# Full-precision routing from whole transposed tokens, per-tile gather evacuation, and query/key heads with tokens on partitions, in a three-block kernel

## The chip, the cores and the metric

One core of a Trainium2 chip runs the whole kernel. The metric is the device time of one launch in microseconds, as a median of several runs.

## The reference

256 tokens of width 1024 pass through a hybrid block with experts, then two layers of feed-forward, mixer, feed-forward. What the change touches:

```python
# routing: top-1 of 4 groups, top-2 of the 4 experts in it (h = rms_norm(x), logits in float32)
grp_p = softmax(t @ wr_g + br_g);  grp_w, grp_idx = top_k(grp_p, 1)
in_grp = (t @ wr_e + br_e) picked by group;  top_l, top_e = top_k(in_grp, 2)
# rwkv mixer: within a chunk of 128 tokens a unit triangular system is solved (a matrix inverse per head)
# last mixer (16 heads of 64): q = rms_norm(q) * g_q / 8;  k = rms_norm(k) * g_k
s = q @ k.T + cum[t] - cum[s]          # cum: running sum of log_sigmoid(forget logit)
o = softmax(masked s) @ v;  o = o * sigmoid(gate);  out = o @ w_out
```

## The kernel before

Five engines run hand-written instruction lists, tied by semaphores. TensorE (PE) does the matmuls, VectorE (DVE) and ScalarE (ACT) evacuate PSUM and prepare operands, SyncE (SP) issues the weight stream, GpSimd (POOL) computes the reciprocal roots of the norms. Tokens are two tiles of 128; 1024 channels are 8 blocks of 128.

**Weights.** A unit is 128 x 2048 floats (1 MB) in a ring of five buffers. Where a product uses fp32r operands, each unit is split into a rounded high part (ACT, L759) and the rest (DVE, L1205), and each product is three matmuls: high x high, low x high, high x low. `split_channels` (L1991) gives channels on partitions, `split_tokens` (L2030) tokens on partitions; both take 48 matmuls of 256 columns per unit. Plain fp32 products are used elsewhere; in the trace each fp32 matmul is two records.

**Norms.** For each stage and token tile, DVE makes F = X times the gain (L1249, or L1247 with the root), PE transposes it (`x_turn`, L2006), ACT copies the result as `h_hi` (L814), DVE subtracts to `h_lo` (L1260). For the projections the first matmul waits for that.

**Routing** (`sparse`). PE multiplies the split router weights with `h_hi` and `h_lo`, 24 matmuls with 256 token columns, into 20 rows (L2281). ACT copies, PE transposes back (L2286), DVE adds the bias (L1559) and finds the group (to L1517). PE counts ranks (L2290 to L2294), DVE builds the slot matrix ST (L1585, L1586) and goes on to the expert choice; ACT takes two exponentials (L959, L961). Tokens are sorted into 5 tiles of 128 slots: 4 groups and one overflow tile. The gather (L2306) multiplies the halves of F (`f_hi` L954, `f_lo` L1554) by ST, 256 slots (two tiles) at a time, into banks 0 to 3; ACT and DVE evacuate both tiles of the first gather at once (L943, L1533).

**Experts.** Each tile takes 8 steps of gate and up (L2318 to L2320), Silu (ACT L970), product (DVE L1622), transpose (L2344) and down (L2333 to L2335). Per-slot weights come from PE by L2376 and are copied by DVE (L1615) after weight splits 2 and 3; the first Silu waits for them.

**The inverse.** 16 matrices of 128 x 128 in 4 groups are inverted in 6 levels, 24 jobs of 4 matrices. A job n does Q = Y M (`q_in`, L2592), masked by DVE (L1811), then M Q (`mw_in`, L2603) and, for n < 20, the transposed product for W (L2605); DVE subtracts both (L1819 for W, L1820 for M) and adds one tap of a convolution (L1780) per period. ACT is free there.

**The last mixer.** PE computes values with tokens on partitions (units c8 to c11, L2030), queries and keys with channels on partitions (c0 to c7, L1991). For each unit ACT squares (L1149) and copies (L745), PE sums the squares over heads with a matmul by a 0/1 matrix (`head_sums`, L2534), ACT takes the root (L1137), DVE the reciprocal over 128 x 512 (L1884) and the product (L1887). The forget logits (L2045 near 1705) follow the second query unit. Then 19 attention slots, one head each: scores (L2739, L2740), mask and maximum on DVE (L1938 to L1942), exponential on ACT (L1169), division on DVE (L1948 to L1952), transposes (L2748), values (L2758, L2759). A quarter of a gate unit, 12 matmuls (L2719), is put between slots. Units are guarded by `proj_free` (bank read) and `side_free` (bank 7 read).

## Time and profile before

| | us |
|---|---|
| median of 3 runs | 2071.33 (2067.37 to 2072.9) |
| the profiled execution | 2068.54 |
| its span | 2066.6 |
| PE, DVE, ACT busy | 1955.6, 1174.9, 868.8 |

Durations below are of the one profiled execution. "PEclk" is the granted clock of PE, 1.00 for 2.4 GHz and 0.50 for 1.2 GHz. A record's duration includes PE's pipeline, so the pace is read from the starts of neighbours.

### The profile page before, as it was taken

What the parts mean: (1) busy time and instruction counts of PE and PEld (TensorE: products, weight loads), DVE (VectorE), ACT (ScalarE), POOL (GpSimd) and SP (SyncE); (2) the same over time, 40 slices, a digit from 0 to 9 for tenths busy, and PEclk for the clock granted to TensorE, in tenths of its full rate; (3) what the DMA queues carried; (4) which work ended last, traced back from release to release, by engine and by line L of the source; (5) the groups of instructions that cost most, each with busy time, mean ns of one, the idle gap of its engine ahead of it and who ended that gap; (6) DMA issues with size and microseconds to landing.
All of it is one profiled execution on the core that took longest, in us unless ns stands there. A gap on an engine that the chain in (4) does not pass through costs nothing.

```text
span 2066.6 us, 23979 instructions
## 1 busy us (share of the span) xinstructions
PE 1955.6 (95%) x9978; PEld 1637.5 (79%) x9978; DVE 1174.9 (57%) x1397; ACT 868.8 (42%) x1083; POOL 42.1 (2%) x106
## 2 busy tenths in 40 slices
PE   6999999799999997999998989999999989999998
PEld 6987768678888885888888977888788878677887
DVE  4314353479888896554358834545655458645454
ACT  4313330257667674444221043444544345324443
POOL 0020000000000000000000000000000000000000
PEclk9989999899999998999999999999999989999999
DMA  8332223459899896555240004555455443107551
GB/s 342 140 123 102 86 98 143 170 222 370 327 345 344 342 350 226 186 194 187 82 143 22 1 1 182 205 186 192 179 194 186 155 151 123 61 2 274 183 183 41
DMA packets 51227, 363.76 MB, mean 176 GB/s; under 512 B 5680, under 2 KB 5808, under 8 KB 8496
## 3 DMA queue, kind: packets, MB, share of 16 engines
q1 hardware_dynamic: 50976, 360.13, 47.1%
q10 hardware_dynamic: 144, 2.10, 0.3%
q8 instruction: 80, 1.31, 0.2%
q14 instruction: 27, 0.22, 0.0%
HBM read 361.15 MB, written 1.05 MB: 175 GB/s over the span
## 4 chain that ended last, share of the span: by engine, by line
PE 86%; DVE 8%; ACT 3%; issue 1%; DMA 0%; POOL 0%; SPq 0%; POOLq 0%; DVEq 0%; ACTq 0%
PE bank L2045 8%; PE bank L2422 7%; PE bank L2424 7%; PE bank L2423 7%; PE bank L1991 5%; PE bank L2257 4%; PE bank L2447 4%; PE bank L2449 4%; PE bank L2448 4%; PE bank L2318 3%; PE bank L2320 3%; PE bank L2319 3%; PE bank L2247 3%; PE bank L2333 2%; PE bank L2335 2%; DVE w_a L1205 2%
## 5 line engine op out<-in xcount | busy, mean ns | idle before, releaser
L1205 DVE TENSOR_TENSOR w_a<-ring,w_a 128x2048 fp32r<-128x2048 f32 x221 | 504.4, 2290 | 301.6 <-ACT w_a L759 300.9
L759 ACT ACTIVATE w_a<-ring 128x2048 fp32r<-128x2048 f32 x221 | 420.6, 1912 | 162.5 <-PE bank L2449 90.7
L2422 PE MATMUL bank<-w_a,h 128*128 128x512 f32 x536 | 214.3, 400 | 11.1 <-DVE h L1260 5.6
L2424 PE MATMUL bank<-w_a,h 128*128 128x512 f32 x536 | 210.2, 392 | 0.0
L2423 PE MATMUL bank<-w_a,h 128*128 128x512 f32 x536 | 209.9, 392 | 0.0
L2045 PE MATMUL bank<-H,ring 128*128 128x256 f32 x800 | 182.6, 385 | 0.0
L1205 DVE TENSOR_TENSOR w_b<-ring,w_b 128x2048 fp32r<-128x2048 f32 x62 | 142.0, 2291 | 66.1 <-ACT w_b L759 65.5
L2045 PEld LDWEIGHTS bank<-H,ring 128*128 128x128 f32 x800 | 151.2, 192 | 26.0 <-issue 5.8
L759 ACT ACTIVATE w_b<-ring 128x2048 fp32r<-128x2048 f32 x62 | 118.6, 1913 | 45.7 <-PE bank L2449 25.8
L1991 PE MATMUL bank<-h,w_a 128*128 128x256 f32 x960 | 121.6, 289 | 7.0 <-DVE h L1260 7.0
L2422 PEld LDWEIGHTS bank<-w_a,h 128*128 128x128 f32 x536 | 101.4, 189 | 33.7 <-DVE hid L1652 6.7
L1991 PEld LDWEIGHTS bank<-h,w_a 128*128 128x128 f32 x960 | 118.3, 195 | 10.7 <-DVE h L1260 7.4
L1006 ACT ACTIVATE sil<-bank,tiny 128x256 f32<-128x256 f32 x88 | 41.8, 475 | 185.3 <-PE bank L2424 185.3
L2424 PEld LDWEIGHTS bank<-w_a,h 128*128 128x128 f32 x536 | 101.3, 189 | 21.8
L2423 PEld LDWEIGHTS bank<-w_a,h 128*128 128x128 f32 x536 | 101.7, 190 | 20.0
L745 ACT ACTIVATE arena<-bank 128x512 f32<-128x512 f32 (+2 forms) x59 | 34.0, 576 | 168.9 <-PE bank L2045 90.5
L2447 PE MATMUL bank<-w_a,hid 128*128 128x512 f32 x264 | 103.2, 391 | 0.0
L2449 PE MATMUL bank<-w_a,hid 128*128 128x512 f32 x264 | 102.8, 389 | 0.0
L2448 PE MATMUL bank<-w_a,hid 128*128 128x512 f32 x264 | 102.7, 389 | 0.0
L2318 PE MATMUL bank<-w_a,xg 128*128 128x512 f32 x244 | 98.1, 402 | 1.5 <-DVE xg L1533 1.5
L2320 PE MATMUL bank<-w_a,xg 128*128 128x512 f32 x244 | 95.8, 392 | 0.0
L2319 PE MATMUL bank<-w_a,xg 128*128 128x512 f32 x244 | 95.6, 392 | 0.0
(455 smaller groups left out, 3293.2 us busy)
## 6 DMA issues: line engine op xcount, KB each, us to landing
ring<-in_stream SPq DMA_DIRECT2D x330, 1024.0 KB, 4.9
G<-in_gains SPq DMA_DIRECT2D x15, 512.0 KB, 5.7
arena<-in_cmp_w ACTq DMA_DIRECT2D x1, 2048.0 KB, 7.9
sm<-in_small SPq DMA_DIRECT2D x1, 1582.0 KB, 13.0
con<-in_consts SPq DMA_DIRECT2D x1, 1384.0 KB, 17.7
X<-in_x SPq DMA_DIRECT2D x2, 512.0 KB, 4.0
out_x<-X SPq DMA_DIRECT2D x2, 512.0 KB, 2.6
sm<-in_small SPq DMA_DIRECT2D x1, 666.5 KB, 22.7
```

Source lines behind the costliest of these rows:

```text
L759: act.activation(w_slot(unit)[:, 0, :], ring[:, unit % RING, :], ACT.Copy).then_inc(S("w_hi"), 1)
L1205: dve.tensor_tensor(w_slot(unit)[:, 1, :], ring[:, unit % RING, :], w_slot(unit)[:, 0, :].bitcast(FP32), ALU.subtract).then_inc(S("w_lo"), 1)
L1991: ins = pe.matmul(ps, w(wp, k), xp[:, k, :], start=(a == 0 and k == 0), stop=(a == 2 and k == terms - 1))
L2045: ins = pe.matmul(ps, weights(k), src[:, k, :], start=(k == 0), stop=(k == KD - 1))
L2318: pe.matmul(bank[4][:, :], x_hi, w[0][:, k, :], start=(half == 0 and k == 0), stop=False)
L2320: ins = pe.matmul(bank[4][:, :], x_lo, w[0][:, k, :], start=False, stop=(half == 1 and k == 3))
L2422: pe.matmul(bank[4 + t][:, :], x_hi, w[0][:, k, :], start=first, stop=False)
L2423: pe.matmul(bank[4 + t][:, :], x_hi, w[1][:, k, :], start=False, stop=False)
L2424: ins = pe.matmul(bank[4 + t][:, :], x_lo, w[0][:, k, :], start=False, stop=end)
L2447: pe.matmul(ps, x_hi, w[0][:, f, d], start=(s == 0 and f == 0), stop=False)
L2448: pe.matmul(ps, x_hi, w[1][:, f, d], start=False, stop=False)
L2449: return pe.matmul(ps, x_lo, w[0][:, f, d], start=False, stop=(s == last and f == 1))
```

## The change

Names and lines are those of the kernel before.

- `keep_busy(n)` issues n fp32 matmuls of the identity into bank 1. Sixteen follow the first transposes; two stand on each side of the second tile's transposes in routing, eight ahead of the rank matmuls, six ahead of the gather; eight stand on each side of the second tile's transposes in the last mixer.
- Routing: ACT and DVE evacuate the transposed tokens in plain fp32 into `h_route`. For each token tile 8 fp32 matmuls with 20 columns give the logits with tokens on partitions; the split router weights, the copy and the transposes back are gone. `f_hi` and `f_lo` swap places in memory and are made within the norm.
- The first gather is evacuated tile by tile: tile 0 ahead of the first expert step, tile 1 after split 3 on ACT and ahead of splits 2 and 3 on DVE. DVE's copy of the slot weights also moves ahead of these splits. ACT runs a Silu on one column after the second exponential, ahead of the gather copies.
- Inverse: the product for W is replaced by four transposes of M (`w_in`), one job later, which ACT copies (`w_turned`); DVE's subtraction for W is gone.
- Last mixer: queries and keys by `split_tokens`; DVE sums squares over 64 columns into 8 values per tile row, ACT takes the root of 128 x 8, DVE the reciprocal, DVE scales out of PSUM into `q_tok`, PE turns 4 blocks (`turn_heads`), ACT copies with the gain. The forget logits move ahead of value unit c10, and their Exp and Ln into the value units. The factor 0.5 moves into the evacuation of the values, the sign into the maximum. Gate quarters 0 and 1 move behind the first scores, the last head unit is turned in slot 1, slots 1 and 2 hold two quarters, split 15 comes one slot later.

The core of the diff:

```diff
-        with nc.sbuf_tensor("f_lo", [P, TT, D], F32R) as f_lo:
+        with nc.sbuf_tensor("f_hi", [P, TT, D], F32R) as f_hi:
             pass
         H = sb("H", [P, KD, T])
-        with nc.sbuf_tensor("f_hi", [P, TT, D], F32R) as f_hi:
+        with nc.sbuf_tensor("f_lo", [P, TT, D], F32R) as f_lo:
...
+        with nc.sbuf_tensor("h_route", [P, KD, T], FP32) as h_route:
...
+                    if name == "moe":
+                        pre_sums(name, t)
+                        act.wait_ge(S("hs"), 2 * NB["moe"] + t + 1)
+                        act.activation(f_hi[:, t, :], F[:, t, :], ACT.Copy).then_inc(S("f_hi"), 1)
+                        act.wait_ge(S("x_turned"), 4 * NB["moe"] + 2 * t + 1)
+                        act.activation(h_route[:, 0:4, t * P:(t + 1) * P], tiles(bank[turn_bank("moe", t, 0)][:, :], 4), ACT.Copy)\
+                           .then_inc(S("x_route"), 1)
...
                     act.wait_ge(S("gathered"), 4 * max(i - 1, 0) + n + 1)
-                    src = bank[n][:, :].rearrange("p (k b c) -> p k b c", k=2, b=2)
-                    bufs = range(2) if i == 0 else (i % 2,)
-                    for b in bufs:
-                        half = b if i == 0 else int(i > 2)
-                        ins = act.activation(xg[:, b, 0, 2 * n:2 * n + 2, :], src[:, :, half, :], ACT.Copy)
-                    ins.then_inc(S("gat_hi"), 1)
+                    if i == 1:
+                        act.wait_ge(S("gat_lo"), n + 1)
+                    src = bank[n][:, :].rearrange("p (k b c) -> p k b c", k=2, b=2)[:, :, int(i in (1, 3, 4)), :]
+                    act.activation(xg[:, i % 2, 0, 2 * n:2 * n + 2, :], src, ACT.Copy).then_inc(S("gat_hi"), 1)
...
-                act.wait_ge(S("unit_used"), D_UNITS["w_out"] + SQUARE)
-                for t in range(TT):
-                    act.activation(f_hi[:, t, :], F[:, t, :], ACT.Copy).then_inc(S("f_hi"), 1)
-                act.wait_ge(S("route_pe"), AT["lg_full"])
-                act.activation(lg_t[0:20, :], bank[7][0:20, 0:T], ACT.Copy).then_inc(S("route_act"), 1)
                 split_at(2)
                 act.wait_ge(S("route_dve"), AT["rt_1"])
                 act.activation(g_exp, g_exp, ACT.Exp).then_inc(S("route_act"), 1)
                 act.wait_ge(S("route_dve"), AT["rt_2"])
                 act.activation(w2, w2, ACT.Exp).then_inc(S("route_act"), 1)
+                act.activation(sil_m[:, 0:1], C("ones")[:, 0:1], ACT.Silu)
                 for n in range(4):
                     gather_hi(0, n)
                 split_at(3)
+                for n in range(4):
+                    gather_hi(1, n)
...
+            for n in range(N_INV - 4):
+                act.wait_ge(S("w_full"), n + 1)
+                act.activation(mat_w[:, 4 * (n % 4):4 * (n % 4) + 4, :], tiles(bank[5 + n % 2][:, :], 4), ACT.Copy)\
+                   .then_inc(S("w_turned"), 1)
...
+            def turned_out(n):
+
+                act.wait_ge(S("side_full"), SI[f"hs{n}"] + 1)
+                act.activation(fq[:, 2 * n:2 * n + 2, :], tiles(bank[7][:, :], 2), ACT.Copy,
+                               scale=(qg8 if n < 4 else P2("kg"))[:, 0:1]).then_inc(S("side_free"), 1)
+
             for n in range(8):
                 split_ahead("c", 4 + n, C_SPLIT)
-
                 act.wait_ge(S(FULL[f"c{n}"][0]), FULL[f"c{n}"][1])
                 if n >= 2:
-                    act.wait_ge(S("side_full"), SI[f"hs{n - 2}"] + 1)
+                    act.wait_ge(S("qk_ss"), n - 1)
                 act.activation(f_sq[:, n % 2, :], bank[5 + GI[f"c{n}"] % 2][:, :], ACT.Square).then_inc(S("f_sq"), 1)
-                evac(f"c{n}", fq[:, 2 * n:2 * n + 2, :], ACT.Copy)
                 if n:
-                    head_norm(n - 1)
-                if n == 3:
-                    act.wait_ge(S("f_dve"), AT["f_abs"])
-                    act.activation(fe[0:N_FOX, :], fa[0:N_FOX, :], ACT.Exp, scale=-1.0).then_inc(S("f_act"), 1)
-                if n == 4:
-                    act.wait_ge(S("f_dve"), AT["f_one"])
-                    act.activation(fl[0:N_FOX, :], fa[0:N_FOX, :], ACT.Ln).then_inc(S("f_act"), 1)
-            head_norm(7)
+                    turned_out(n - 1)
+                act.wait_ge(S("qk_ss"), n + 1)
+                act.activation(qk_rs[:, n % 2, :], qk_ss[:, n % 2, :], ACT.Sqrt, bias=C("eps")[:, 0:1], scale=1.0 / HD)\
+                   .then_inc(S("qk_root"), 1)
...
+            def route_in(t):
+
+                if t == 1:
+                    low_tokens(0)
+                dve.wait_ge(S("x_turned"), 4 * NB["moe"] + 2 * t + 2)
+                dve.tensor_copy(h_route[:, 4:8, t * P:(t + 1) * P], tiles(bank[turn_bank("moe", t, 1)][:, :], 4))\
+                   .then_inc(S("x_route_2"), 1)
+                if t == 1:
+                    low_tokens(1)
+
+            def low_tokens(t):
+
+                if t == 0:
+                    dve.wait_ge(S("unit_used"), D_UNITS["w_out"] + SQUARE)
+                dve.wait_ge(S("f_hi"), t + 1)
+                dve.tensor_tensor(f_lo[:, t, :], F[:, t, :], f_hi[:, t, :].bitcast(FP32), ALU.subtract).then_inc(S("f_lo"), 1)
...
+                for n in range(4):
+                    gather_lo(1, n)
+                dve.wait_ge(S("route_pe"), AT["rc_full"])
+                dve.tensor_copy(rc, bank[7][:, 0:6 * N_TILES]).then_inc(S("route_dve"), 1)
                 split_at(2)
                 split_at(3)
-                dve.wait_ge(S("route_pe"), AT["rc_full"])
-                dve.tensor_copy(rc, bank[7][:, 0:6 * N_TILES]).then_inc(S("route_dve"), 1)
...
-                if n < N_INV - 4:
-                    dve.tensor_tensor(mat_w[:, four, :], mat_w[:, four, :], tiles(bank[5 + n % 2][:, :], 4), ALU.subtract)
...
+            def squares_in(n):
+
+                dve.wait_ge(S("f_sq"), n + 1)
+                dve.tensor_reduce(qk_ss[:, n % 2, :], f_sq[:, n % 2, :].rearrange("p (h d) -> p h d", d=HD), AX.X, ALU.add)\
+                   .then_inc(S("qk_ss"), 1)
+
+            def scaled_out(n):
+
+                rs = qk_rs[:, n % 2, :]
+                dve.wait_ge(S("qk_root"), n + 1)
+                link(dve.reciprocal(rs, rs))
+                if n >= 2:
+                    dve.wait_ge(S("side_full"), SI[f"hs{n - 2}"] + 1)
+                heads = lambda x: x.rearrange("p (h d) -> p h d", d=HD)
+                dve.tensor_tensor(heads(q_tok[:, n % 2, :]), heads(bank[5 + GI[f"c{n}"] % 2][:, :]),
+                                  rs.unsqueeze(2).to_broadcast([P, 8, HD]), ALU.mult).then_inc(S("proj_free"), 1)
...
-            for n in range(2, 14):
-                split("c", n)
-                if n == 7:
-                    forget_1()
-                if n >= 7:
-                    head_norm(n - 7)
-                if n == 9:
-                    forget_2()
-                if n == 11:
+            split("c", 2)
+            split("c", 3)
+            forget_1()
+            split("c", 4)
+            forget_2()
+            split("c", 5)
+            for n in range(8):
+                squares_in(n)
+                split("c", 6 + n)
+                scaled_out(n)
+                if n == 1:
                     forget_3()
...
-                    dve.tensor_reduce(neg_max[:, 2 * b:2 * b + 1], fat_s[:, b, 0:P], AX.X, ALU.max)
-                    link(dve.tensor_reduce(neg_max[:, 2 * b + 1:2 * b + 2], fat_s[:, b, P:3 * P], AX.X, ALU.max))
-                    dve.tensor_scalar(neg_max[:, 2 * b:2 * b + 2], neg_max[:, 2 * b:2 * b + 2], -1.0, None, ALU.mult)\
+                    dve.tensor_reduce(neg_max[:, 2 * b:2 * b + 1], fat_s[:, b, 0:P], AX.X, ALU.max, negate=True)
+                    dve.tensor_reduce(neg_max[:, 2 * b + 1:2 * b + 2], fat_s[:, b, P:3 * P], AX.X, ALU.max, negate=True)\
                        .then_inc(S("fmax_ok"), 1)
...
-                    link(dve.tensor_scalar(inv, inv, 0.5, None, ALU.mult))
...
+            def keep_busy(count):
+
+                for _ in range(count):
+                    pe.matmul(bank[1][:, 0:P], C("ident"), C("ident"), start=True, stop=True)
+
             pe.wait_ge(S("con_id"), 16)
             for t in range(TT):
                 x_turn("proj", t)
+            keep_busy(16)
...
+            def logits(t):
+
+                pe.wait_ge(S("x_route"), t + 1)
+                pe.wait_ge(S("x_route_2"), t + 1)
+                for k in range(KD):
+                    ins = pe.matmul(bank[2 * t][:, 0:20], h_route[:, k, t * P:(t + 1) * P], route_w[:, k, :],
+                                    start=(k == 0), stop=(k == KD - 1))
+                ins.then_inc(S("route_pe"), 1)
+
+            logits(0)
+            keep_busy(2)
             x_turn("moe", 1)
+            keep_busy(2)
+            logits(1)
 
             def sparse():
 
                 m0 = D_UNITS["moe"]
-                pe.wait_ge(S("h_lo"), HI0["moe"] + 4)
-                pe.wait_ge(S("wr_lo"), 1)
-                for a, (wp, x) in enumerate(((0, h_hi), (1, h_hi), (0, h_lo))):
-                    for k in range(KD):
-                        ins = pe.matmul(bank[7][0:20, 0:T], w_r2[:, wp, k, :], x[:, k, :], start=(a == 0 and k == 0),
-                                        stop=(a == 2 and k == KD - 1))
-                ins.then_inc(S("route_pe"), 1)
-                pe.wait_ge(S("route_act"), AT["lg_t"])
-                for t in range(TT):
-                    ins = pe.transpose(bank[6][:, 20 * t:20 * t + 20], lg_t[0:20, t * P:(t + 1) * P], C("ident")[0:20, 0:20])
-                ins.then_inc(S("route_pe"), 1)
+                keep_busy(8)
...
+                keep_busy(6)
...
+                if n >= 4:
+                    pe.wait_ge(S("w_turned"), n - 3)
                 if n >= 2:
                     pe.wait_ge(S("mw_ok"), n - 1)
                 for i in range(4):
                     q = mat_q[:, n % 2, i * P:(i + 1) * P]
                     ins = pe.matmul(bank[2 + n % 2][:, i * P:(i + 1) * P], mat_w[:, 4 * g + i, :], q, start=True, stop=True)
-                    if n < N_INV - 4:
-                        ins = pe.matmul(bank[5 + n % 2][:, i * P:(i + 1) * P], q, mat_w[:, 4 * g + i, :], start=True,
-                                        stop=True)
                 ins.then_inc(S("mw_full"), 1)
+
+            def w_in(n):
+                pe.wait_ge(S("mw_ok"), n + 1)
+                if n >= 2:
+                    pe.wait_ge(S("w_turned"), n - 1)
+                for i in range(4):
+                    ins = pe.transpose(bank[5 + n % 2][:, i * P:(i + 1) * P], mat_m[:, 4 * (n % 4) + i, :], C("ident"))
+                ins.then_inc(S("w_full"), 1)
...
+                if 2 <= n < N_INV - 2:
+                    w_in(n - 2)
...
+            keep_busy(8)
             x_turn("c", 1)
+            keep_busy(8)
             pe.wait_ge(S("h_lo"), HI0["c"] + 4)
             for n in range(2):
                 split_tokens(bank[5 + GI[f"c{8 + n}"] % 2], "c", n, range(1, 2))
+            pe.wait_ge(S("h_32"), H32["c"] + 4)
+            ps = side_begin("f")
+            w_f = P2("w_f").rearrange("p (k n) -> p k n", k=KD)
+            project(ps[0:N_FOX, 0:T], lambda k: w_f[:, k, :]).then_inc(S("side_full"), 1)
             for n in range(2, 4):
                 split_tokens(group_begin(f"c{8 + n}"), "c", n)
+
+            def turn_heads(n):
+
+                ps = side_begin(f"hs{n}")
+                pe.wait_ge(S("proj_free"), GI[f"c{n}"] + 1)
+                for c in range(2):
+                    for t in range(TT):
+                        at = t * UC + c * P
+                        ins = pe.transpose(ps[:, c * T + t * P:c * T + (t + 1) * P], q_tok[:, n % 2, at:at + P], C("ident"))
+                ins.then_inc(S("side_full"), 1)
+
             for n in range(8):
-                split_channels(group_begin(f"c{n}"), "c", 4 + n)
-                if n == 1:
-                    pe.wait_ge(S("h_32"), H32["c"] + 4)
-                    ps = side_begin("f")
-                    w_f = P2("w_f").rearrange("p (k n) -> p k n", k=KD)
-                    project(ps[0:N_FOX, 0:T], lambda k: w_f[:, k, :]).then_inc(S("side_full"), 1)
+                split_tokens(group_begin(f"c{n}"), "c", 4 + n)
                 if n:
-                    head_sums(f"hs{n - 1}", f_sq[:, (n - 1) % 2, :], "f_sq", n)
+                    turn_heads(n - 1)
...
+                if n == 1:
+                    turn_heads(7)
+                if n in (1, 2):
+                    gate_quarter(2 * n - 1)
+                    gate_quarter(2 * n)
+                elif n < 14:
+                    gate_quarter(n + 2 if n else 0)
```

## Rows read from the trace of the kernel before

**Rows 1.** The page: its head and the busy time of each engine.
```profile
span 2066.6 us, 23979 instructions
...
PE 1955.6 (95%) x9978; PEld 1637.5 (79%) x9978; DVE 1174.9 (57%) x1397; ACT 868.8 (42%) x1083; POOL 42.1 (2%) x106
```

**Rows 2.** PE's waits over the span: total us, times, longest us.
```profile
PE bank L2748 <- DVE sm L1952: 5.7, 3, 4.4
```

**Rows 3.** Timeline of PE at the start: start, us, line, tiles, count, [idle before].
```profile
19.51 13.76 PE L1991 MATMUL bank<-h,w_a 128*128 128x256 f32 x96 [7.04 <-DVE h L1260]
33.11 11.68 PE L2030 MATMUL bank<-w_a,h 128*128 128x256 f32 x96
```

**Rows 4.** Timeline of one period of the inverse, PE and DVE.
```profile
1121.39 1.06 PE L2592 MATMUL bank<-arena 128*128 128x128 f32 x8
1121.63 0.68 DVE L1819 TENSOR_TENSOR arena<-arena,bank 128x512 f32<-128x512 f32 x1
...
1124.07 1.06 PE L2592 MATMUL bank<-arena 128*128 128x128 f32 x8
```

**Rows 5.** Timeline of PE in the expert stage: ten transposes.
```profile
440.50 1.25 PE L2390 MATMUL bank<-con,ST 128*128 128x128 f32 x10
```

**Rows 6.** Timeline of PE: fp32 matmuls with 24 moving columns.
```profile
100.15 3.75 PE L2052 MATMUL bank<-sm,H 128*128 128x24 f32 x32
```

**Rows 7.** Timeline of all engines through routing.
```profile
398.69 1.22 PE L2006 MATMUL bank<-con,F 128*128 128x128 f32 x8 [2.64 <-DVE F L1249]
...
401.36 5.22 PE L2281 MATMUL bank<-h,late 128*20 128x256 f32 x24 [1.45 <-DVE h L1260]
...
407.38 0.38 DVE L1559 SCALAR_TENSOR_TENSOR sm<-bank,tiny,sm 128x20 f32<-128x20 f32 x2 [2.46 <-PE bank L2286]
...
408.59 0.17 DVE L1517 TENSOR_TENSOR sm<-sm 128x8 f32<-128x8 f32 x1
...
413.94 0.20 ACT L961 ACTIVATE sm<-sm 128x2 f32<-128x2 f32 x1 [3.62 <-DVE sm L1593]
...
419.65 0.50 PE L2318 MATMUL bank<-w_a,xg 128*128 128x512 f32 x1 [1.54 <-DVE xg L1533]
```

**Rows 8.** The chain that ended last, in order of time: the gather.
```profile
411.91 6.22 PE bank L2306 x32
```

**Rows 9.** Windows: PE, PEld, DVE, ACT, POOL busy (count), PEclk, DMA share, GB/s.
```profile
410.00:415.00 5.00, 3.36 (x15) 3.18 (x15) 3.78 (x21) 1.17 (x5) 0.00 (x0) 0.50 0.00 0
...
430.00:435.00 5.00, 4.83 (x15) 3.93 (x16) 2.46 (x3) 3.99 (x3) 0.00 (x0) 0.66 0.17 70
```

**Rows 10.** Timeline of the first expert step, ACT and PE.
```profile
427.76 1.28 ACT L970 ACT_TABLE_LOAD   x1 [7.15 <-PE bank L2320]
...
430.17 0.66 PE L2344 MATMUL bank<-con,mid_m 128*128 128x128 f32 x2 [2.49 <-DVE mid_m L1622]
```

**Rows 11.** Timeline of PE in the last mixer.
```profile
1674.43 19.76 PE L2030 MATMUL bank<-w_a,h 128*128 128x256 f32 x144 [2.17 <-DVE h L1260]
...
1716.99 6.31 PE L1991 MATMUL bank<-h,w_a 128*128 128x256 f32 x48
...
1723.60 6.31 PE L1991 MATMUL bank<-h,w_a 128*128 128x256 f32 x48
...
1749.57 1.02 PE L2534 MATMUL bank<-arena,con 128*128 128x512 f32 x2
...
1821.92 1.69 PE L2719 MATMUL bank<-h,w_a 128*128 128x256 f32 x12
...
1826.89 1.69 PE L2719 MATMUL bank<-h,w_a 128*128 128x256 f32 x12
```

**Rows 12.** Groups by form, DVE in the last mixer: busy us, mean ns | idle.
```profile
L1884 DVE RECIPROCAL arena<-arena 128x512 f32<-128x512 f32 x8 | 26.8, 3348 | 3.4 <-ACT arena L1137 3.4
```

**Rows 13.** Windows of the end of the inverse, columns as in rows 9.
```profile
1172.00:1176.00 4.00, 2.89 (x22) 2.32 (x20) 3.96 (x8) 0.00 (x0) 0.00 (x0) 1.00 0.00 0
1176.00:1180.00 4.00, 3.15 (x17) 3.11 (x18) 3.86 (x10) 0.24 (x1) 0.00 (x0) 0.72 0.01 4
```

86 lines of the change are left out of this document (35 added, 51 removed).

## The prediction

> **What bounds the kernel now.** I read the page first, then who TensorE (PE) waited for, then the stretches that the diff touches, instruction by instruction. PE is busy 1955.6 of 2066.6 us [rows 1], 95%, so two things can shorten the kernel: fewer PE instructions where PE never pauses, and fewer or warmer pauses where it does. Weight splitting on ScalarE (ACT) and VectorE (DVE) fills the feed-forward and expert stages, but PE hardly waits there, and the diff leaves their steady state alone. The edits lie in five places: the first projection, routing, the first expert tile, the triangular inverse in the second mixer, and queries and keys plus the attention start in the last mixer. In the last one DVE is late: PE waits 5.7 us for one DVE line [rows 2].
>
> **Prices used everywhere.** At the full clock a 128x256 fp32r matmul is issued every 0.12 us (96 in 11.68) [rows 3]. An fp32 matmul of 128 columns appears as two records of 0.112 us: in the inverse 24 records take 2.68 us [rows 4]. A transpose of 128 columns is one record, 10 in 1.25 us with the drain, 0.11 each [rows 5]. A 24-column fp32 matmul is also two records, 32 in 3.75 us with the drain, 0.11 each [rows 6]. At the half clock a 256-column matmul takes 0.22 us (24 in 5.22) [rows 7], and so does a 128-column fp32 record (estimate, twice 0.112).
>
> **The first projection.** 16 filler matmuls are put between the transposes and the wait for the split input. PE sat idle 7.04 us there and then ran 96 matmuls in 13.76 us where the next 96 took 11.68 [rows 3]: 2.1 us went to a half-speed start. The fillers take 16 x 0.22 = 3.6 us at full clock and 16 x 0.43 = 6.9 us at half clock, both inside the 7.04, so they delay nothing. Whether the clock stays up across the rest of the wait (up to 3.4 us) is open; the bounds are 0 and -2.1. I take **-1.5**.
>
> **Routing.** Before, after the second token tile's transposes at 398.69, PE waits for the split, issues 24 matmuls at half clock (401.36, 5.22 us), a copy and a transpose follow, and DVE has logits at 407.38 [rows 7]. After, tile 0's logits come in the shadow before 398.69: 16 records x 0.11 = 1.8 us from the end of the projection, and two fillers. For tile 1 ACT squares X (1.05 us) and copies F (1.0) while PE transposes, then evacuates a half (0.6); DVE subtracts one tile of F (1.2), evacuates the other half (0.6) and is done at 400.6. Eight matmuls take 1.8 us, so logits are there at 402.7 instead of 407.38: -4.6. The copies of F, once 2 us behind the transposes on ACT, are thereby moved ahead of ACT's evacuation; DVE's second subtraction sits behind its own evacuation and ends before the logits. The eight fillers before the rank matmuls end at 404.5; the group choice, 1.4 us after the first logits op in both kernels, is ready at about 404.1, so they cost 0.4. The rank matmuls and the slot comparison, 3.3 us from 408.59 [rows 7] to 411.91 [rows 8], give 407.3 for the start of the gather (-4.6). Six more fillers (1.3 us) lie in the slot comparison's 1.6 us.
>
> **Gather and first step.** The gather is 32 matmuls in 6.22 us from 411.91 [rows 8], mostly at half clock (0.50 over 410 to 415 [rows 9]); at full clock it is 32 x 0.12 = 3.7 us and ends at 411.0. Evacuation of one tile, not two, halves each copy. But a load of the Silu table (1.28 us, as at 427.76 [rows 10]) now stands on ACT between the weight exponential and the gather copies. The exponential ran at 413.94, 2.0 us after the gather's start [rows 7]; so 409.3, table to 410.9, four copies of 0.33 to 412.3, DVE's last subtraction 412.7. The first expert matmul, at 419.65 before [rows 7], comes at 412.8: **-6.9**. Then the second tile's four evacuations, and the weights' copy, stand ahead of two weight splits on DVE (2.2 us each). These splits end at 422.5, and the product DVE owes PE is behind them at 423.0; PE's transposes come 10.2 us after the first expert matmul, where they came 10.5 after it (430.17 against 419.65 [rows 7, 10]). So the moved table load buys only another 0.3 there: DVE is late next in ACT's place. DMA issue resumes some 3 us later relative to PE; its cover is the full ring, by which the DMA engines were busy for only 0.17 of 430 to 435 [rows 9]; without that cover up to 3 us come back. Sum for routing and the first step: **-7.1**, bounds -4 (fillers and gather at half clock) and -9.5 (the half-clock phase after 430 also goes).
>
> **The inverse.** A period is 24 records, 2.68 us (1121.39 to 1124.07), and DVE is full as well, with 0.60 for the W subtraction in it (1121.63) [rows 4]. After: 8 + 8 records and 4 transposes, 20 x 0.112 = 2.23; DVE 2.71 - 0.60 = 2.11; ACT one 0.6 us copy, for which it has no other work. PE becomes the bound by 0.12. That is 0.45 x 19 periods = 8.5, plus 8 records at half clock in the first (1.7), less 4 records added in one late period (0.45), plus 0.6 because DVE no longer trails PE at the end: **-10.4**. The new wait (W of job n-4 turned and copied) has two periods of room for 0.6 + 0.2 us. Bounds: -7.5 (half the DVE saving lost to hand-overs) and -11.5.
>
> **Last mixer.** (a) Eight fillers on either side of the second tile's transposes. 144 matmuls took 19.76 us [rows 11], 17.3 at 0.12: -2.4. The fillers take 1.8 us and the wait ended by the split lasts 2.17 us [rows 11] and the one ahead of the transposes about as long, so no delay. (b) A unit of queries or keys costs 48 x 0.12 in either form; the fp32 sum over 512 columns (2 records of 0.42) becomes four transposes (0.45). Units start every 6.60 us before [rows 11] and every 6.2 after; with the forget-gate stall of 0.5 gone that is -3.0. Hidden: DVE's reduce 0.7 + split 2.2 + reciprocal 0.2 + product 0.7 + waits, 4.8 us, inside PE's next unit of 5.76; it was 3.35 for a wide reciprocal, 0.75 and 2.2 [rows 12]. (c) From the end of the eighth unit (1749.57) to that of the last gate quarter (1826.89 + 1.6) PE took 79.0 us [rows 11], with one wait of 4.4 for DVE in it [rows 2], a shorter one for a split before, and some 5 us at half clock behind them. After: slot 0 costs 0.45 + 3.6, slots 1 and 2 5.5 each (two quarters, the last head turn), then 11 slots of 4.97 [rows 11]: 69.7, so -9.3. What was late there was DVE: two reciprocals of 3.35 us and two splits before the third slot. Now DVE takes up slot 0 at +4.9 us, while PE has 9.6 us of work before its next demand on it. Dropping two 0.17 us operations per slot counts only at the end, 0.3. Sum: **-15.1**, bounds -10 ((c) only half) and -17.
>
> **Sum.** -1.5 - 7.1 - 10.4 - 15.1 = -34.1. The profiled execution took 2068.5 (span 2066.6 and 1.9 around it), giving 2034.4; the median of the shown runs is 2.8 above that execution, giving 2037.2. I forecast **2036**.
>
> **A rule against it.** The granted clock fell after 1176 (0.72 over 1176 to 1180), behind gaps of PE, while 1172 to 1176, with PE at 2.89 of 4 us, ran at 1.00 [rows 13]. The Trainium skill, TensorE: Matmul & The Clock Gate, part 4 (PE-mode transpose), says that transposes don't count as TensorE activity in the same way as matmuls; by it the inverse would show less activity than its busy share. No row here has a long mix of transposes and matmuls, so the trace neither confirms nor refutes it.
>
> **Rivals.**
> 1. Fillers don't hold the clock (0.25 with the attention start good). Then the first projection gives 0, routing -4, (a) nothing: 1.5 + 3.1 + 2.4 = 7 us less gain, **2043**. For it: fillers and 20-column matmuls load PE lightly, and no row shows a clock held by such. Against: pauses shrink to under 1 us.
> 2. The attention start stays late (0.15): the new chain Square, reduce, root, reciprocal, product, turn spans three engines and one split, and if one link exceeds 5.8 us each unit stalls, and DVE reaches slot 0 late. (c) is lost: **2045**; with rival 1, 2052 (0.05).
> 3. Slower (0.03): the inverse falls to half clock and stays there. Matmuls are then 16 of its 20 records, 1.79 of 2.23 us, 80% against the 72% of 1172 to 1176 that kept 1.00 [rows 13]; it decides if transposes count for nothing and 80% is too little. Twenty periods of 20 x 0.22 instead of 2.23 us cost 43, so **2079**.
> 4. Clock luck all the way, the phase after 430 included (0.07): **2029**.
> The change could also fail to do what it says (PE bound by DVE in the inverse, so no gain from fewer records), but DVE loses 0.60 there too; it is in the bound of -7.5.
>
> **Chances.** Forecast 0.45 (2031 to 2041), rivals 0.25, 0.15, 0.05, 0.03, 0.07. The range 2028 to 2049 leaves out rivals 3 and the double case and a little of each end. Against 2071.3, faster by over 0.3% (about what a measurement can tell from no change) means under 2065: 0.94; same 0.03; slower 0.03.
>
> **What would show it.** Logits ready 4 us or so after F; 32 gather matmuls in under 4 us at clock 1.0; expert stage starting 6.9 us earlier relative to F; inverse period 2.23 on PE; unit period 6.2; no wait of PE for DVE in the first four attention slots. Wrong if fillers end after what they wait beside, if the inverse shows 0.5, or if new waits for ACT's copies appear.

## The result and the profile after

The changed kernel takes 2040.84 us (median; single executions 2036.78 to 2044.43) against 2072.11 us for the kernel before beside it (2067.37 to 2077.0): a ratio of 0.9847, 95% interval 0.9821 to 0.9873, so 1.3 to 1.8% or 26 to 37 us faster. The forecast was 2036, with 2028 to 2049. The profiled execution has a span of 2042.6 us and stands near the upper end of its kernel, as the profiled one of before stood near the lower end of its own.

The page of the changed kernel: head and busy time, as [rows 1].

```profile
span 2042.6 us, 24047 instructions
...
PE 1953.9 (96%) x10020; PEld 1641.3 (80%) x10020; DVE 1136.5 (56%) x1350; ACT 874.3 (43%) x1098; POOL 43.0 (2%) x106
```

PE's busy time has hardly changed: it includes the fillers. DVE has lost 38 us. The rows below are timelines of the changed kernel (start, duration, engine, line, operation, tiles, count and, in brackets, the idle time before and who ended it). First projection, against [rows 3]:

```profile
12.43 4.55 PE L2099 MATMUL bank<-con 128*128 128x128 f32 x32
19.57 13.25 PE L2016 MATMUL bank<-h,w_a 128*128 128x256 f32 x96 [2.58 <-DVE h L1269]
32.65 11.68 PE L2055 MATMUL bank<-w_a,h 128*128 128x256 f32 x96
```

Routing, gather and first expert step, against [rows 7, 8, 10]:

```profile
404.49 1.09 PE L2031 MATMUL bank<-con,F 128*128 128x128 f32 x8 [0.41 <-DVE F L1258]
...
408.42 0.24 DVE L1577 SCALAR_TENSOR_TENSOR sm<-bank,tiny,sm 128x20 f32<-128x20 f32 x1 [0.84 <-PE bank L2310]
...
412.92 0.38 PE L2342 MATMUL bank<-ST,f_hi 128*128 128x256 f32 x1 [0.20 <-DVE ST L1604]
...
415.17 1.28 ACT L962 ACT_TABLE_LOAD   x1
...
418.51 0.50 PE L2354 MATMUL bank<-w_a,xg 128*128 128x512 f32 x1 [1.24 <-DVE xg L1556]
```

A period of the inverse, against [rows 4]; L2651 is the four transposes, L1101 ACT's copy:

```profile
1122.54 1.06 PE L2630 MATMUL bank<-arena 128*128 128x128 f32 x8
1123.44 1.06 PE L2643 MATMUL bank<-arena 128*128 128x128 f32 x8
1124.33 0.60 PE L2651 MATMUL bank<-con,arena 128*128 128x128 f32 x4
...
1124.97 0.60 ACT L1101 ACTIVATE arena<-bank 128x512 f32<-128x512 f32 x1 [1.63 <-PE bank L2651]
```

The last mixer, against [rows 11]: L2763 turns a finished query or key unit.

```profile
1697.79 6.00 PE L2055 MATMUL bank<-w_a,h 128*128 128x256 f32 x48
1703.62 0.60 PE L2763 MATMUL bank<-con,arena 128*128 128x128 f32 x4
1703.98 6.00 PE L2055 MATMUL bank<-w_a,h 128*128 128x256 f32 x48
1711.35 0.63 PE L2763 MATMUL bank<-con,arena 128*128 128x128 f32 x4 [1.38 <-DVE arena L1913]
...
1736.15 0.60 PE L2763 MATMUL bank<-con,arena 128*128 128x128 f32 x4
...
1804.34 1.69 PE L2778 MATMUL bank<-h,w_a 128*128 128x256 f32 x12
```

The 4.4 us wait for DVE's division [rows 2] is gone; the one wait that is new is the 1.38 us before the transposes at 1711.35.

**Stages.** The program is the same in all but the edited places, so one can read each stage as the distance between two PE instructions that every kernel has. All distances are in us, from the starts in the PE timeline of each kernel's one trace. The medians and ratios come from all its executions. From the third row on the kernels are those of the experiments below. P: first matmul of the projection to the next group. R: second tile's transposes in routing to the gather. G: gather to the first expert matmul. A: first to second transposes of the second mixer. I: first job of the inverse to the first product behind it. M: second transposes of the last mixer to the first of the next stage.

| kernel | median | ratio (95%) | P | R | G | A | I | M |
|---|---|---|---|---|---|---|---|---|
| before | 2072.11 | | 13.6 | 13.2 | 7.7 | 9.1 | 73.8 | 191.1 |
| changed | 2040.84 | 0.9847 (0.9821 to 0.9873) | 13.1 | 8.4 | 5.6 | 11.9 | 63.1 | 176.7 |
| whole_again | 2043.91 | 0.9865 (0.9846 to 0.9885) | 13.1 | 10.1 | 5.6 | 12.0 | 63.3 | 177.9 |
| routing_alone | 2065.70 | 0.9962 (0.9949 to 0.9976) | 13.4 | 8.4 | 5.6 | 11.9 | 74.1 | 190.9 |
| inverse_alone | 2061.24 | 0.9943 (0.9926 to 0.9959) | 13.5 | 13.2 | 8.5 | 11.9 | 63.0 | 190.9 |
| mixer_alone | 2053.94 | 0.9920 (0.9903 to 0.9937) | 13.0 | 13.1 | 8.2 | 11.9 | 73.7 | 176.7 |
| quarters_only | 2068.61 | 0.9993 (0.9978 to 1.0009) | 13.4 | 13.1 | 8.4 | 11.9 | 73.9 | 190.8 |
| turn_by_matmul | 2048.85 | 0.9891 (0.9865 to 0.9918) | 13.1 | 11.0 | 5.2 | 11.9 | 72.4 | 176.7 |
| splits_first | 2042.63 | 0.9864 (0.9844 to 0.9883) | 13.1 | 8.4 | 5.6 | 11.9 | 63.0 | 176.7 |
| no_preload | 2037.29 | 0.9852 (0.9833 to 0.9870) | 13.1 | 8.4 | 5.3 | 9.1 | 62.1 | 176.8 |
| no_fillers | 2048.23 | 0.9889 (0.9872 to 0.9906) | 14.0 | 10.8 | 7.1 | 11.9 | 63.0 | 178.8 |
| no_fillers_again | 2051.23 (one) | | 14.1 | 10.7 | 7.3 | 11.9 | 63.0 | 178.8 |
| filled_gaps | 2036.24 | 0.9836 (0.9818 to 0.9853) | 11.6 | 10.9 | 5.3 | 9.1 | 61.6 | 176.7 |
| mended | 2030.15 | 0.9802 (0.9781 to 0.9822) | 11.6 | 11.0 | 5.2 | 9.1 | 61.8 | 175.2 |

The kernel before had a median of 2072.45 beside whole_again and the three `_alone` kernels, of 2068.53 beside no_fillers, filled_gaps, no_preload and splits_first, and of 2071.97 beside mended, turn_by_matmul, quarters_only and no_fillers_again. Medians should be compared within such a set.

### The profile page after: what moved, and what is told of

Same layout as the page of the kernel before. It is cut to its first block, busy times and chain, and to the rows that moved or that the text cites. A ratio compares the mean times of both kernels' runs of the same rounds, so it can differ in the third digit from the quotient of the medians.

```text
span 2042.6 us, 24047 instructions
## 1 busy us (share of the span) xinstructions
PE 1953.9 (96%) x10020; PEld 1641.3 (80%) x10020; DVE 1136.5 (56%) x1350; ACT 874.3 (43%) x1098; POOL 43.0 (2%) x106
## 4 chain that ended last, share of the span: by engine, by line
PE 75%; DVE 6%; ACT 3%; issue 1%; POOL 0%; POOLq 0%; DVEq 0%; ACTq 0%
PE bank L2460 8%; PE bank L2462 8%; PE bank L2461 8%; PE bank L2288 4%; PE bank L2487 4%; PE bank L2485 4%; PE bank L2486 4%; PE bank L2070 3%; PE bank L2354 3%; PE bank L2356 3%; PE bank L2355 3%; PE bank L2278 3%; PE bank L2055 3%; PE bank L2369 2%; PE bank L2371 2%; PE bank L2370 2%
## 5 line engine op out<-in xcount | busy, mean ns | idle before, releaser
L746 ACT ACTIVATE arena<-bank 128x512 f32<-128x512 f32 (+2 forms) x51 | 29.2, 573 | 172.5 <-PE bank L2070 91.8
L2055 PE MATMUL bank<-w_a,h 128*128 128x256 f32 x672 | 85.0, 288 | 2.6 <-DVE h L1269 2.6
L1672 DVE SCALAR_TENSOR_TENSOR hid<-bank,tiny,sil 128x256 f32<-128x256 f32 x88 | 42.3, 480 | 80.6 <-ACT sil L1009 80.6
```

## Experiments

**1. Each part by itself, and the whole once more.** The three parts of the diff are separate edits: inverse_alone has those of the inverse, mixer_alone those of the last mixer with its fillers, routing_alone those of routing, gather and first expert step with theirs.

```diff
 # inverse_alone, on the kernel before
-                    if n < N_INV - 4:
-                        ins = pe.matmul(bank[5 + n % 2][:, i * P:(i + 1) * P], q, mat_w[:, 4 * g + i, :], start=True,
-                                        stop=True)
...
+                if 2 <= n < N_INV - 2:
+                    w_in(n - 2)
```

> The kernel before with the new inverse alone (transposes and ScalarE's copies in place of the second product). Theory A (TensorE is bound by its records there): the period falls from 2.68 to 2.23 us, 19 times, and the kernel gains 8 to 11.5 us. Rival (transposes count less, the clock falls to the half): the granted clock shows 0.5 in the middle of the inverse, and the kernel loses some 30 us or more. Rival (the new wait for ScalarE's copy binds): period of 2.4 us or more with idle time of TensorE ahead of the products, gain below 5 us.

> The kernel before with the new last mixer alone, its sixteen filler matmuls included. Theory A: unit period 6.2 instead of 6.60 us, no wait of TensorE for VectorE in the first attention slots, the stretch from the end of the eighth unit to the last gate quarter 9 us shorter, first 144 matmuls in 17.3 us: gain 13 to 17 us. Rival (attention start stays late): units start every 6.2 us but TensorE still waits 4 us or more before the third slot: gain 6 to 9 us.

> The kernel before with routing, gather and first expert step changed alone, fillers there included, none elsewhere. Theory A: from the second token tile's transposes to the first expert matmul 14.0 us instead of 20.96, the gather in 3.7 to 4.1 us: gain 5 to 9 us. Rival (fillers do not hold the clock): the gather at clock 0.5 takes over 5.5 us, gain 3 to 4 us.

Measured: 11.2 (inverse_alone), 18.5 (mixer_alone) and 6.8 us (routing_alone) less than the kernel before beside them. The stages touched show 10.8 (I), 14.3 (M) and 6.9 (R and G, 14.0 instead of 21.0). Theory A holds for inverse_alone and routing_alone. For mixer_alone it holds in the trace, but the gain of the medians lies 1.5 us above its range, and no trace shows where the 4 us beyond M are: of the 15.2 us between the two profiled executions M accounts for 14.3. The three gains add up to 36.5 us, while whole_again, measured beside them, gained 28.5. So a median of some executions is no better than a few us as the price of one part, and the stages are the better measure. The 40 us in the middle of the new inverse in inverse_alone, as windows (busy time of PE, PEld, DVE, ACT, POOL with counts, granted clock, DMA share, GB/s):

```profile
1125.00:1165.00 40.00, 40.00 (x362) 40.00 (x361) 38.81 (x73) 10.75 (x18) 0.00 (x0) 1.00 0.01 1
```

The granted clock is 1.00, that is 2.4 GHz, all through, and so it is in the changed kernel over the same window; rival 3 is out.

> The changed kernel once more, unaltered. The profiled execution of it took 10 us more than my sum gives for it, and nearly all of that lies in stretches whose code the change does not touch (100 to 118, 300 to 310, 372 to 376, 790 to 806 and 997 to 1004 us), where TensorE ran at the half clock and did not in the profile of before. Theory A (chance: which of these stretches are slow differs from execution to execution of one kernel): in the new profile at least two of the five are at the full clock, the times of single executions spread over 7 us or so (2036 to 2044), and the gain over before is 28 to 36 us. Theory B (the change shifts the work and thereby slows these places each time): the same five stretches are slow again, within a microsecond, and the gain is 24 to 28 us.

The changed kernel again took 2037.66 to 2045.44 us. These are windows over some stretches whose code is the same in every kernel (columns as above); first the changed kernel's first trace, then its second. By 1000 us the second trace is 8 us ahead, so that its stretch for 997 to 1004 is 989 to 997 (also at half clock, not shown).

```profile
102.00:110.00 8.00, 8.00 (x43) 8.00 (x44) 0.00 (x0) 0.21 (x1) 0.00 (x0) 0.57 0.75 314
372.00:376.00 4.00, 4.00 (x13) 3.17 (x12) 0.47 (x1) 1.91 (x1) 0.00 (x0) 0.57 0.40 160
792.00:806.00 14.00, 8.53 (x25) 6.27 (x24) 7.32 (x9) 4.53 (x8) 2.34 (x6) 0.51 0.00 1
997.00:1004.00 7.00, 6.31 (x31) 5.91 (x30) 2.11 (x3) 3.50 (x8) 1.19 (x4) 0.51 0.00 0
1106.00:1120.00 14.00, 9.60 (x42) 9.13 (x43) 11.50 (x21) 0.00 (x0) 0.00 (x0) 0.51 0.00 1
```

```profile
102.00:110.00 8.00, 8.00 (x69) 8.00 (x69) 0.00 (x0) 0.81 (x2) 0.00 (x0) 1.00 0.70 291
372.00:376.00 4.00, 4.00 (x20) 3.54 (x19) 1.09 (x1) 0.00 (x0) 0.00 (x0) 1.00 0.00 0
792.00:806.00 14.00, 11.64 (x47) 9.38 (x48) 7.06 (x9) 6.43 (x11) 2.32 (x6) 0.77 0.18 66
```

The places of 102, 300 (not shown) and 372 are at full clock this time and that of 792 in part: theory A for those. The same program is at half clock in one execution and at full clock in the next. Over the first of these places that makes 3.0 us (from the 24-column matmuls to the next transposes 25.1 us, then 22.1), and the time from the first projection to routing comes out at 366.4 to 375.3 us over the fourteen traces. That of 997 is slow again, as theory B said, but not because the change shifts the work: the stage A is 11.9 or 12.0 in every trace of a kernel without fillers ahead of it but two, before's and no_preload's, with 9.1, and 11.9 in quarters_only, whose code is the old one up to the last mixer. So the trace of before, on which the forecast rests, was lucky there by 2.8 us.

**2. Who sets the period of the inverse.**

```diff
-                    ins = pe.transpose(bank[5 + n % 2][:, i * P:(i + 1) * P], mat_m[:, 4 * (n % 4) + i, :], C("ident"))
+                    ins = pe.matmul(bank[5 + n % 2][:, i * P:(i + 1) * P], mat_m[:, 4 * (n % 4) + i, :], C("ident"), start=True,
+                                    stop=True)
```

> The changed kernel with the four transposes per job of the inverse issued as fp32 matmuls by the identity: the same data, 8 records instead of 4, VectorE's and ScalarE's part unchanged. Theory A (TensorE's records set the period): the period is 24 records, 2.68 us, and the whole gain of the inverse but what VectorE's end gives is lost, 8 us slower than the changed kernel. Rival (taking the subtraction off VectorE is what shortened the period): 2.3 us or so, within 2 us of the changed kernel.

The timeline of PE, and of DVE as far as it waits:

```profile
1130.79 1.06 PE L2630 MATMUL bank<-arena 128*128 128x128 f32 x8
1131.68 1.06 PE L2643 MATMUL bank<-arena 128*128 128x128 f32 x8
1131.94 0.69 DVE L1831 TENSOR_TENSOR arena<-bank,con 128x512 f32<-128x512 f32 x1 [0.36 <-DVE arena L1800]
1132.58 1.06 PE L2651 MATMUL bank<-con,arena 128*128 128x128 f32 x8
...
1133.47 1.06 PE L2630 MATMUL bank<-arena 128*128 128x128 f32 x8
```

The period is 2.68 us again (1130.79 to 1133.47), and DVE now has an idle 0.36. The stage is 72.4 us, 9.3 more than with transposes and 1.4 less than before. PE's records set the period. The 1.4 lie behind the last period, and not all of them are DVE's: 0.55 are a shorter wait for DVE (the last two of the products M Q start 1.57 us apart, in the kernel before 2.12), and 0.8 come from the stage's last 16 small matmuls, which take 2.00 us at full clock and took 2.87 in the kernel before, where the clock fell during them [rows 13]. What else the freed DVE time is worth is room: DVE has 2.71 us of work in a period before, and with that much it could not follow a period of 2.23.

**3. The start of the attention.** The new order of the gate's quarters on the kernel before (split 15, one slot later, is not shown):

```diff
-            gate_quarter(0)
-            gate_quarter(1)
...
-                if n < 14:
-                    gate_quarter(n + 2)
+                if n in (1, 2):
+                    gate_quarter(2 * n - 1)
+                    gate_quarter(2 * n)
+                elif n < 14:
+                    gate_quarter(n + 2 if n else 0)
```

> The kernel before with the changed order of the gate's quarters and of the last weight split alone (two quarters behind the first scores, two each in slots 1 and 2); queries, keys and their roots as before. Theory A (the wide reciprocals and splits make VectorE late, not the order): TensorE still waits 3 us or more for VectorE in the first four slots and the stretch from the last unit to the next stage's transposes shortens by less than 3 of 10.5 us. Rival (the order does it): no wait above 1 us, and 6 us or more of the 10.5.

```profile
1765.21 0.55 PE L2746 MATMUL bank<-con,sm 128*128 128x128 f32 x3 [0.44 <-DVE sm L1952]
1765.52 3.12 PE L2719 MATMUL bank<-h,w_a 128*128 128x256 f32 x24
1773.63 0.90 PE L2746 MATMUL bank<-con,sm 128*128 128x128 f32 x3 [2.92 <-DVE sm L1952]
```

PE still waits 0.44 and 2.92 us for the division in the second and third slots, and M is 190.8: the order alone is worth 0.3 of 14.4 us. The 3 us that the expectation asked for a single wait was just missed, but the gain is nowhere near the rival's 6 us: DVE was late. (No run has the new queries and keys with the old order, so whether they need the new one is open.) DVE's groups in the changed last mixer (busy, mean ns) show what went, against 3348 ns each in [rows 12]:

```profile
L1902 DVE TENSOR_REDUCE tiny<-arena 128x8 f32<-128x512 f32 x8 | 5.4, 680 | 18.7 <-ACT arena L1161 18.7
L1909 DVE RECIPROCAL tiny<-tiny 128x8 f32<-128x8 f32 x8 | 1.6, 194 | 0.0
```

**4. First expert step.** Once the early Silu is left out, once DVE's order is put back:

```diff
 # no_preload
-                act.activation(sil_m[:, 0:1], C("ones")[:, 0:1], ACT.Silu)
 # splits_first
+                split_at(2)
+                split_at(3)
                 for n in range(4):
                     gather_lo(1, n)
                 dve.wait_ge(S("route_pe"), AT["rc_full"])
                 dve.tensor_copy(rc, bank[7][:, 0:6 * N_TILES]).then_inc(S("route_dve"), 1)
-                split_at(2)
-                split_at(3)
```

> The changed kernel without the one-column Silu ahead of the gather's evacuation. Theory A (the load of the table, 1.28 us, only changes places, and VectorE is late next anyway): the first expert matmul comes 0.6 to 1.0 us earlier, the first transposes of the experts stay within 0.5 us of where they were relative to the gather, total within 1.5 us of the changed kernel. Rival (the load on ScalarE is on the path of the first product): the first transposes come 1.3 us later relative to the gather.

> The changed kernel with VectorE's two weight splits again ahead of the second tile's subtractions and of the copy of the per-slot weights. Theory A (the first Silu waits for that copy, so the order decides): the first transposes of the experts come 1 to 2.5 us later relative to the gather, and so does all behind them. Rival (VectorE's sum of work ahead of the product is the same in either order): the first transposes stay within 0.5 us.

The first Silu of the experts (in no_preload the table load ahead of it), what ACT waited for there, and the first transposes, in the changed kernel, in splits_first and in no_preload:

```profile
428.20 0.47 ACT L973 ACTIVATE sil_m<-bank,tiny 128x256 f32<-128x256 f32 x1 [7.55 <-PE bank L2356]
...
429.31 0.44 PE L2380 MATMUL bank<-con,mid_m 128*128 128x128 f32 x2 [1.21 <-DVE mid_m L1642]
```

```profile
428.36 0.47 ACT L973 ACTIVATE sil_m<-bank,tiny 128x256 f32<-128x256 f32 x1 [7.57 <-PE bank L2356]
...
429.48 0.44 PE L2380 MATMUL bank<-con,mid_m 128*128 128x128 f32 x2 [1.21 <-DVE mid_m L1642]
```

```profile
420.00 1.28 ACT L972 ACT_TABLE_LOAD   x1 [7.30 <-PE bank L2355]
...
422.41 0.58 PE L2379 MATMUL bank<-con,mid_m 128*128 128x128 f32 x2 [2.49 <-DVE mid_m L1641]
```

From the gather's start to these transposes: 16.39 us, 16.42 with the splits first, 17.40 without the early load. So the order on DVE is worth nothing here (theory A of that run fell, its rival holds): in the changed kernel the Silu waits for PE's own gate and up matmuls, not for the weights' copy. The early load is worth 1.0 us net, 1.3 at the first Silu less 0.3 at the first expert matmul; there the rival was nearer than theory A. That no_preload is yet the quicker of the two by its median (2037.29 against 2042.63 for splits_first beside it) is not explained by its edit: in its one trace the stages A (9.1) and I (62.1), which it doesn't touch, are shorter.

All three have PE at the half clock during the gate and up matmuls (the changed kernel from 424 to 427 us, granted clock 0.50). In the two traces without fillers of experiment 5 these matmuls run at full clock, and there the order of arrival turns round. The same place in no_fillers:

```profile
428.23 0.47 ACT L973 ACTIVATE sil_m<-bank,tiny 128x256 f32<-128x256 f32 x1 [5.75 <-PE bank L2356]
429.79 0.48 DVE L1642 SCALAR_TENSOR_TENSOR mid_m<-bank,tiny,sil_m 128x256 f32<-128x256 f32 x1
430.32 0.44 PE L2380 MATMUL bank<-con,mid_m 128*128 128x128 f32 x2 [2.19 <-DVE mid_m L1642]
```

The Silu is done at 428.7, but DVE comes out of its second split only at 429.8, without a pause, and the transposes come 10.2 us after the first expert matmul. In the changed kernel DVE waits 0.49 us for the Silu. So DVE is late at full clock, and what no_preload and splits_first show holds for the half clock only; neither was tried at full clock.

**5. The fillers.**

```diff
-                for _ in range(count):
+                for _ in range(0):
```

> The changed kernel with all its filler matmuls left out, all else equal. Theory A (the fillers hold the clock where they stand, and lie in waits): the gather and the last mixer's first 144 matmuls come back to the half clock in most executions (1.2 to 3.4 us each), the first projection loses 0.5 us: 3 to 6 us slower than the changed kernel, at 2044 to 2050. Rival (the clock falls or holds there by chance, whether or not fillers stand in the gaps): within 1.5 us of the changed kernel, 2040 to 2044, and a similar number of half-clock stretches in routing and in the last mixer.

> The changed kernel without fillers once more, for a second trace. Theory A (they hold the clock where they stand): the gather again takes 6 us or more from its start's own wait to the first expert matmul (7.1 us instead of 5.6), and a half-clock stretch follows the transposes of the last mixer. Rival (chance): at least one of the two places is at the full clock this time.

Without fillers G is 7.1 and 7.3, M 178.8 both times; with them G is 5.2 to 5.6 in eight traces of eight, M 176.7 or 176.8 in six of the seven with the changed kernel's mixer. P is 13.0 to 14.1 in the seven traces without the sixteen at the start and 13.1 in the five with them. That is theory A, at two executions without. Of the 1.5 us that the fillers win in G, 0.6 are lost right behind it: the half-clock stretch that stands 10 us later without them now meets the gate and up matmuls, and the first transposes come 10.8 instead of 10.2 us after the first expert matmul. R is mixed: 8.4 in four traces with fillers, 10.1 to 11.0 in four, 10.7 and 10.8 without. Against splits_first beside it, whose stages match the changed kernel's, no_fillers is 5.6 us slower by the medians (the intervals of their ratios, from 0.9872 and up to 0.9883, overlap a little).

Where R is 10.9 or 11.0, the clock fell during the fillers, and the fillers themselves came too late. In turn_by_matmul:

```profile
405.16 2.88 PE L2099 MATMUL bank<-con 128*128 128x128 f32 x16
...
409.83 2.91 PE L2099 MATMUL bank<-con 128*128 128x128 f32 x12
...
411.28 0.28 DVE L1604 TENSOR_SCALAR ST<-sm 128x128 fp32r<-128x128 f32 x1
...
412.39 0.56 PE L2342 MATMUL bank<-ST,f_hi 128*128 128x256 f32 x1
```

The slot matrix was ready at 411.56, the gather started 0.8 us later, behind twelve records that take 1.58 us at full clock (411.13 in the changed kernel). filled_gaps and mended show the same.

**6. More of them.** filled_gaps puts fillers where PE waits longest (the second argument is the bank that they write):

```diff
-            keep_busy(16)
+            keep_busy(26)
...
                 scatter(N_TILES - 1)
+                keep_busy(18, 4)
                 x_turn("ffn0", 0)
...
+                    keep_busy({"ab": 8, "c": 15}.get(then, 0), 4)
                     x_turn(then, 0)
...
+            keep_busy(14, 4)
             pe.wait_ge(S("gram_free"), N_MAT)
...
+                if n == 1:
+                    keep_busy(11, 4)
...
+            keep_busy(19, 4)
             pe.wait_ge(S("gn_y"), 1)
...
+            keep_busy(22, 4)
             pe.wait_ge(S("y_rw"), 1)
```

> The changed kernel with further fillers in the longest waits of TensorE that have none: 10 more ahead of the first projection, 18 after the experts, 8 and 15 ahead of the first transposes of the second and last mixer, 14 and 11 around the first job of the inverse, 19 and 22 ahead of the mixer's output. In every trace so far a half-clock stretch follows these waits (792 to 806, 997 to 1004, 1106 to 1120, 1222 to 1236, 1649 to 1656 us in the changed kernel: 3.4 to 8.5 us each at the half clock or twice that long). Theory A (a wait makes the clock fall, a filled wait doesn't): most of them go, 10 to 20 us faster than the changed kernel, 2022 to 2032. Rival (fillers of 128 columns are too light, or the clock falls anyway): no change of the stretches and 0 to 3 us slower through fillers that end late.

mended moves the 19 behind the transposes that follow and cuts the forget gate's DVE work in two:

```diff
+                if n == 1:
+                    forget_3a()
+                if n == 2:
+                    forget_3b()
```

> The changed kernel with the further fillers of the run before, the 19 that stood too early (they ran for 4.4 us while the wait they were for, 5.1 us, lay behind the next transposes) moved behind those transposes, and with VectorE's forget-gate arithmetic cut in two, one half after the second and one after the third query unit. Theory A: the mixer from the inverse's end to the next transposes comes back to 83 to 84 us, the wait of 1.38 us for VectorE before the third unit's transposes goes, no half-clock stretch at 792 to 806, 997 to 1004, 1106 to 1120 and 1649 to 1656: 2029 to 2034. Rival (what the fillers gain in one place is lost in another, since the clock falls somewhere anyway): 2035 to 2040.

Windows of mended over the places after the filled waits, and its start (timeline):

```profile
790.00:806.00 16.00, 12.58 (x75) 10.39 (x74) 8.79 (x10) 6.31 (x11) 3.08 (x8) 1.00 0.17 51
988.00:1006.00 18.00, 16.09 (x139) 15.36 (x138) 5.80 (x8) 5.08 (x11) 2.63 (x8) 1.00 0.02 4
1098.00:1113.00 15.00, 12.74 (x110) 12.19 (x110) 14.62 (x27) 1.20 (x2) 0.00 (x0) 1.00 0.00 1
```

```profile
12.44 6.70 PE L2104 MATMUL bank<-con 128*128 128x128 f32 x52
19.65 11.78 PE L2021 MATMUL bank<-h,w_a 128*128 128x256 f32 x96 [0.51 <-DVE h L1269]
```

The clock is 1.00 where the changed kernel's two traces have the half clock for much of the time. filled_gaps gains 32.3 us over the kernel before beside it. That is 6.4 more than splits_first, but only 1.0 more than no_preload in the same set, and its median of 2036.24 lies outside theory A's range; the interval of its ratio overlaps the changed kernel's, so that its gain over the changed kernel is not clear of noise. It is less than theory A's 10 to 20: with the 19 misplaced fillers the way from the inverse's end to the next stage's transposes takes 87.5 us for 84.4, and half-clock stretches at 1157 to 1164 and 1854 to 1857 (granted clock in its trace) take some back. mended, at 0.9802, beats both kernels: the one before by 42 us beside it, the changed one by 10.7 us on medians of different sets of runs (the intervals of the ratios, up to 0.9822 and from 0.9821, just meet). It has both the moved fillers and the cut DVE work, and only the latter has a price of its own, the 1.6 us of M. Its time lies in theory A's range; of the stretches that theory A said would go, one at 1642 to 1646 stays in part, and the mixer's end stage did not come back to 84 (84.8). The wait before the third unit's transposes is gone, and M falls to 175.2.

## Why the prediction was right, point by point

- **First projection, -1.5:** 0.5 in the changed kernel, and as much on the mean of the traces without these fillers. The assumption that failed is that the clock would outlast the last 2.6 us of the wait. It was still 1.00 as the matmuls began and 0.50 over 21 to 24 us. With 26 fillers and 0.5 us left, the 96 matmuls took 11.78 us and the gain is 2.0: the bound of -2.1 was right for that dose.
- **Routing to the gather, -4.6:** -4.8 in the profiled execution. Logits came 3.9 us after the second transposes (4.0 said), the gather 8.4 (8.6 said). But in four of the eight traces with these fillers the clock falls between 402 and 413 us and R is 10.1 to 11.0, no better than the 10.7 and 10.8 without fillers. That is rival 1 in part, and in three of them its sign too, fillers that end after what they wait beside. The mean is 9.6, so -3.6.
- **Gather and first step:** first expert matmul 6.9 us earlier relative to the second transposes, as said. The gather took 4.36 us with its last record, at granted clock 1.00, not under 4. That DVE is "late next in ACT's place" did not hold in the changed kernel: the splits end at 428.3, the Silu at 428.7, and it waited for PE. The step that failed is the clock of the gate and up matmuls: a half-clock stretch moved from 430 [rows 9] to 424 and now slows them, so that the first transposes came 10.8 us after the first expert matmul and not 10.2, and the table load, taken off that spot, is worth 1.0 and not 0.3. In the two traces without fillers, at full clock, it is 10.2, with DVE late as the prediction had it.
- **Inverse, -10.4:** -10.7 to -10.8. Period 2.23, DVE full at 39 of 40 us but not ahead, ACT idle 1.63 between copies, as said. In turn_by_matmul the terms come apart: 9.3 for PE's records and 1.4 behind the last period, of which 0.55 are DVE's (0.6 said) and 0.8 the clock's, which the sum didn't have.
- **The rule against it:** the granted clock stayed at 1.00 over 1125 to 1165 with four transposes in every twenty records. The Trainium skill, TensorE: Matmul & The Clock Gate, part 4, says that transposes don't count as activity in the same way; no run here shows a stream of this mix lose the clock by it, and turn_by_matmul, with matmuls in place of the transposes, has 1.00 over the same window. With sixteen matmuls in every twenty records the runs don't tell whether transposes count.
- **Last mixer, -15.1** (its parts add up to 15.0): -14.4. Part (c) was 69.8 us (1736.15 to 1804.34 and 1.6) for 69.7 said. The unit period was 6.19 for 6.2 said. The mis-sized term is (b), 1.7 instead of 3.0: the forget gate's DVE work, 5.6 us with its reciprocal, was moved between two units, and PE waits 1.38 us. The prediction let the old stall of 0.5 vanish without asking where that work went. Its spare time was to be read: 18.7 us of idle time over eight units in front of the reduces, 2.3 each, and a product that was 1.6 us early (ended 1701.98, wanted at 1703.62), together 3.9. Part (a) was 2.1 us, also by M without fillers, for 2.4 said. What hid most of the miss in (b) is luck: behind the last gate quarter 1.4 us went where 0.3 were said, since in the kernel before the clock is at 0.51 over 1837 to 1840, in the last slots, and in the changed kernel at 1.00 there. In whole_again it fell there again (not shown), and M is 177.9, 1.1 more.
- **Rivals.** Rival 2 did not come. Rival 1 came in part, as told. The chance named as rival 4 is real in both directions.
- **The total, 34.1:** on the means of the traces with and without each edit the stages give 0.5 (P) + 3.6 (R) + 2.8 (G, 8.2 to 5.4) + 10.9 (I) + 14.0 (M), less 0.3 between the first expert matmul and the first transposes: 31.5 us, and the medians differ by 31.3. The forecast was 4.8 us too low. Its terms were 2.6 us too large together: 1.0 for the projection, 1.0 for routing, gather and first step, 1.1 for the mixer, and back 0.5 for the inverse. Another 1.2 is the step from its own sum, 2037.2, to 2036, for which it gives no reason, and 0.8 the kernel before, at 2072.11 instead of 2071.33. That sum and medians agree so closely is partly luck, as single executions of one kernel differ by more.

## What to carry to other kernels

Where one engine is busy for 95% of the span, count its records in each period and its waits at each hand-over; both added up here within 1.1 us per part. When work is moved off one engine's path, write down where it lands and what spare time is there: the only new wait above 0.5 us was a chain moved without that sum. In the projection a wait filled to within half a microsecond kept the clock, the same wait filled for two thirds did not; in routing pauses of 0.4 us and fillers kept it in four traces of eight only. Put the fillers directly behind the last work that doesn't wait and ahead of the instruction that does, and read in the trace that the wait behind them has gone.
